# Modulation vectors on TensorE alone: 384 products with one column in place of GpSimd's multiply and add

## What is computed

```
mod   = silu(c) @ w_mod + b_mod        # two layers, 1024 -> 3072: shift, scale, gate
y     = rms_norm(h, gain) * (1 + scale) + shift
h     = h + gate * branch(y)
```

## Time and profile before

| what | us |
|---|---|
| median of 3 runs | 1314.91 |
| lowest and highest of them | 1311.63, 1318.79 |
| the profiled execution's own time | 1313.33 |
| its span in the trace | 1311.5 |
| TensorE busy | 904.6 (69%) |
| VectorE busy | 830.7 (63%) |
| GpSimd busy | 558.0 (43%) |
| ScalarE busy | 257.5 (20%) |

### The profile page before, as it was taken

The page is one execution under the profiler, slowest core; times in us unless marked ns, Lnnn a source line. Parts: engine busy times, 40 slices in busy tenths (PEclk is TensorE's granted clock), DMA queues, the critical chain, the costliest instruction groups (busy, mean ns, idle before and its releaser), DMA issues. The chain is left out here.

```text
span 1311.5 us, 17486 instructions
## 1 busy us (share of the span) xinstructions
PE 904.6 (69%) x6828; PEld 688.4 (52%) x6828; DVE 830.7 (63%) x1942; ACT 257.5 (20%) x515; POOL 558.0 (43%) x440
## 2 busy tenths in 40 slices
PE   6449979997968889687634454434444499659998
PEld 6449958796756657456411131111211288538887
DVE  1975152237978968595478777777765489972311
ACT  3021101103352213221002111011100143412210
POOL 1858777974433433253244445444444034600000
PEclk9769979997879959788756565555655689869999
DMA  9636547758999999999999999999999414212341
GB/s 382 252 129 252 198 176 288 273 210 341 426 420 384 420 418 414 423 423 421 421 421 421 422 420 421 421 421 418 417 420 421 194 67 175 80 64 71 122 148 45
DMA packets 51266, 401.99 MB, mean 307 GB/s; under 512 B 5616, under 2 KB 7920, under 8 KB 8944
## 3 DMA queue, kind: packets, MB, share of 16 engines
q0 software_dynamic: 40320, 293.62, 54.5%
q1 hardware_dynamic: 10000, 104.57, 20.6%
q10 hardware_dynamic: 864, 2.68, 0.5%
HBM read 399.80 MB, written 1.05 MB: 306 GB/s over the span
## 5 line engine op out<-in xcount | busy, mean ns | idle before, releaser
L409 POOL DMA_INDIRECT arena<-uv_dram,arena x192 | 220.8, 1150 | 322.2 <-PE ps L552 276.4
L552 PE MATMUL ps<-arena 128*32 128x256 f32 x1536 | 157.4, 549 | 213.0 <-DVE arena L1410 213.0
L1394 DVE CUSTOM_DVE_ANT_0 arena<-arena 128x1024 f32<-128x1024 f32 x192 | 232.5, 1225 | 98.0 <-DMA arena<-uv_dram,arena 92.2
L552 PEld LDWEIGHTS ps<-arena 128*32 128x32 f32 x1536 | 51.5, 141 | 301.1 <-DVE arena L1410 255.8
L822 PE MATMUL ps<-xn,wring 128*128 128x256 f32 x640 | 147.6, 395 | 17.5 <-DVE arena L1738 9.9
L822 PEld LDWEIGHTS ps<-xn,wring 128*128 128x128 f32 x640 | 127.1, 199 | 38.0 <-issue 18.2
L458 PE MATMUL ps<-xn,wring 128*128 128x128 f32 x1024 | 129.2, 288 | 10.3 <-DMA wring<-units_dram 6.0
L458 PEld LDWEIGHTS ps<-xn,wring 128*128 128x128 f32 x1024 | 125.1, 203 | 18.6 <-issue 8.6
L409 POOL DMA_INDIRECT wring<-uv_dram,arena x64 | 79.2, 1238 | 108.6 <-PE ps L552 98.6
L941 ACT ACTIVATE gel<-dots 128x2 f32<-128x2 f32 x128 | 26.0, 203 | 471.1 <-DVE dots L1394 446.3
L552 PE MATMUL ps<-wring,arena 128*32 128x256 f32 x512 | 50.4, 530 | 72.6 <-DVE arena L1410 72.6
(11 more groups left out here) (244 smaller groups left out, 1319.0 us busy)
## 6 DMA issues: line engine op xcount, KB each, us to landing
wring<-units_dram SPq DMA_DIRECT2D x48, 2048.0 KB, 9.6
arena<-mod_dram POOLq DMA_DIRECT2D x24, 1024.0 KB, 6.2
arena<-uv_dram,arena POOLq DMA_INDIRECT x192, 14.2
hA<-x_t_dram SPq DMA_DIRECT2D x2, 512.0 KB, 5.4
arena<-mem_t_dram ACTq DMA_DIRECT2D x1, 1024.0 KB, 11.5
arena<-keys_dram ACTq DMA_DIRECT2D x2, 512.0 KB, 4.7
wring<-uv_dram,arena POOLq DMA_INDIRECT x64, 14.3
wring<-grp_dram SPq DMA_DIRECT2D x1, 1024.0 KB, 4.8
```

Of the source, the lines that this page charges most:

```text
L409: pool.indirect_dma_start(ring[b], None, uv_d, bass.IndirectOffsetOnAxis(ap=idx[:, n:n + 1], axis=0)).then_inc(sem(f"row_in{b}"), 16)
L552: mm = pe.matmul(acc_ps(q)[G * c:G * (c + 1), :], lhsT=diag[:, s % 2, j, :], rhs=ring[b][:, D + 256 * c:D + 256 * (c + 1)], start=(p == 0 ...
L1394: post(V.tensor_tensor_reduce(out=ring[b][:, 0:D], in0=ring[b][:, 0:D], in1=x_rep[q % 2], scale=1.0, scalar=0.0, op0=ALU.mult, op1=ALU.add ...
```

## The change

GpSimd no longer multiplies or adds. It issues the loads of the chunks, each as soon as TensorE has summed the chunk two before it, and it waits for the last sum ahead of the first gather. TensorE takes the loaded chunk itself as weights: for each of a chunk's two halves of 128 columns, 8 products (one for each block of channels) with one column of `silu_c`, summed in PSUM. `mod_chunk` comes at the same places as before. `mod_p` is gone.

```diff
-MOD_SUMS = 4
@@
-        mod_p = x_rep[1].rearrange("p (s n) -> p s n", s=MOD_SUMS)
@@ GpSimd
-            need(pool, "silu_c")
-            for i in range(MOD_CHUNKS):
-                w = mod_w[:, i % 2]
-                pool.wait_ge(sem(f"mod_in{i % 2}"), 16 * (i // 2 + 1))
-                did(pool, pool.tensor_tensor(w, w, silu_c[:].unsqueeze(2).broadcast_to([P, KB, 256]), ALU.mult), "pool_step")
-                did(pool, pool.tensor_tensor(w[:, 0:4], w[:, 0:4], w[:, 4:8], ALU.add), "pool_step")
-                did(pool, pool.tensor_tensor(w[:, 0:2], w[:, 0:2], w[:, 2:4], ALU.add), "pool_step")
-                if i >= MOD_SUMS:
-                    need(pool, "mod_sum", i - MOD_SUMS + 1)
-                did(pool, pool.tensor_tensor(mod_p[:, i % MOD_SUMS], w[:, 0], w[:, 1], ALU.add), "mod_part")
-                if i + 2 < MOD_CHUNKS:
-                    pool.dma_start(w.rearrange("p k n -> p (k n)"), mod_d[i + 2]).then_inc(sem(f"mod_in{i % 2}"), 16)
+            for i in range(2, MOD_CHUNKS):
+                need(pool, "mod_sum", i - 1)
+                pool.dma_start(mod_w[:, i % 2].rearrange("p k n -> p (k n)"), mod_d[i]).then_inc(sem(f"mod_in{i % 2}"), 16)
+
+            need(pool, "mod_sum", MOD_CHUNKS)
@@ TensorE, mod_chunk(i)
-                need(pe, "mod_part", i + 1)
+                if i == 0:
+                    need(pe, "silu_c")
+                pe.wait_ge(sem(f"mod_in{i % 2}"), 16 * (i // 2 + 1))
                 for j in range(2):
-                    mm = pe.matmul(ps[:, 7, 2 * i + j:2 * i + j + 1], lhsT=mod_p[:, i % MOD_SUMS, j * P:(j + 1) * P], rhs=cst("one"),
-                                   start=True, stop=True)
+                    for k in range(KB):
+                        mm = pe.matmul(ps[:, 7, 2 * i + j:2 * i + j + 1], lhsT=mod_w[:, i % 2, k, j * P:(j + 1) * P], rhs=silu_c[:, k:k + 1],
+                                       start=(k == 0), stop=(k == KB - 1))
                 post(mm, "mod_sum")
```

## The result

| kernel | median, us | ratio to before (95% interval) | first gather, us | span less first gather |
|---|---|---|---|---|
| before | 1316.9 (4 runs) | | 301.4 | 1010.1 |
| changed | 1381.4 (4 runs) | 1.048 (1.043 to 1.052) | 368.3 | 1009.2 |

The forecast was 1378 us, slower, with 1328 to 1404 as the range. The kernel of before ran again beside every group of runs; ratios are always taken within a group.

A forecast was written before the change was run, and what follows sets the result against it. VectorE, then TensorE bound the path to the first gather, then transfers: -35.7 + 71 - 12.6 - 8.6, plus 2.1 and 0.3, gives +16.5 on 1313.3 (1329.8); clock falls add 47 (1376.8); median 1378 us, range 1328 to 1404.

The forecast's parts named there:

- The frame: Transfer engines bound a gather stage of fixed length; the change only shifts its start, the first gather at 301.35 us.
- Part 1, the relief of VectorE: Before L604: without GpSimd's arithmetic VectorE speeds up, so L604 starts at 56.1 us, 35.7 us won, first chunk included.
- Part 2, the price of a record: TensorE's chunks after the first: 28 more records each at 0.11 us, 71 us added; ends 58 and 135 us.
- The rival of cheap weight loads: 128-column weights load at 0.04 us a record, 644 records cost 26 us for 71: 1286 us; chance of faster 0.04.
- Part 3, the waits: TensorE's waits at L684, L458, L729 and L762 close, 12.6 us; half clock after waits goes too, 8.6 us.
- Part 4, loads and gathers: Chunk loads cost 0, at most 3 us; waiting for the last sum before the first gather adds 2.1 and 0.3 us.
- The sum at full clock: First gather 16.5 us later if the clock holds, 1329.8 us; as a rival, median 1331 us, chance 0.18.
- Part 5, the clock: TensorE's one-column chunks act like pauses: 18 clock falls at 2.6 us add 47 us; ends 31 and 74 us.
- The sign "near 0.75": TensorE's granted clock between 92 us and the first gather, expected well below the earlier 0.95, near 0.75.
- The sign "up to 7 us for a chunk at half clock": TensorE's chunks, expected to take 3.5 us at full clock and up to 7 us at half.

The follow-up runs named there:

- e3: Kernel before, but GpSimd begins its arithmetic only when g is there and TensorE's sums stand three steps later: 1297.1 us, ratio 0.979.
- e6: e1_wide, with GpSimd multiplying and adding five times on a scratch buffer, result unused, from about 28 to 70 us: 1365.3 us, ratio 1.037.
- e5: e1_wide with only the first half of each chunk's columns multiplied, 8 products in place of 16: 1293.8 us, ratio 0.984.
- e1_wide: Changed kernel, each product of the modulation passing 128 equal columns of silu_c in place of one: 1334.9 us, ratio 1.009.
- e2: Changed kernel, each chunk in two halves of 16 one-column records, one half after each step from the seventh on: 1344.4 us, ratio 1.015.
- e7: Kernel before, GpSimd's arithmetic begun at g, chunks 0 and 23 on TensorE (128 equal columns), last two chunks early in TensorE's list: 1290.8 us, ratio 0.977.

## Why the prediction was right, point by point

**The frame.** "A fixed time after its start" held to within 5 us over nine kernels. That made it possible to forecast a 1300 us kernel from one moment at 300 us. The forecast had that moment at 364.9 (301.35 + 16.5 + 47), and it came at 368.3.

**Part 1, the relief of VectorE.** Forecast: L604 at 56.1; measured 56.33. The cause is shown from both sides: e3 moves GpSimd's arithmetic in time, e6 adds it back without any use, and L604's place is at 56.35 in the one and 87.3 in the other. One size was off: I priced the eight L1471 at 4.3 us by L1754, and they took 3.3. It did not matter, since the third convolution waited for its input anyway (2.4 us, above).

**Part 2, the price of a record.** Forecast 0.11, measured 0.109 (a chunk, one column), 0.112 (128 columns) and 0.108 to 0.113 on the path (e5). The rival of cheap weight loads is out.

**Part 3, the waits.** Forecast: 12.6 us close. TensorE's waits in the second part went from 14.5 to 2.6 us, so 11.9 did. L458 kept 0.8 us that I had closed. The forecast gave two reasons, a faster VectorE and a slower TensorE. For the wait of 6.8 us at L684 the first alone is enough: VectorE's short convolution took 13.2 us from 170.8 on in the kernel before, and takes 3.1 from 170.9 on now. For the smaller waits nothing parts the two.

**Part 4, loads and gathers.** Landing took 5.2 us in the median and 7.5 at worst, and no chunk waited for its load. `mod_sum` released the first gather.

**The sum at full clock.** It stood at 317.9 us for the first gather; e1_wide, which is that case, has 320.9. Two of these 3 us are the wider products' own (23 chunks x 0.09 us). The forecast had also taken every half clock of before as gone, and e1 kept a fall of 3.4 us right behind the narrow products near 170 us, with no wait there; it is worth up to 1.7 us.

**Part 5, the clock.** This was the bold part, with 47 of the 64 us, and its two factors were choices: 18 falls at 2.6 us. Measured: 19 falls, 102 us at half speed, so 51 us, 2.7 for each. By e1 the first gather moved 47.4 us; with the wider chunks' 2.1 us and the 1.7 us of the fall that e1 kept that makes 51.2, half of the 102. The assumption that a chunk of short columns acts like a pause, which no row could show, is what e1 and e2 have shown. That both factors came out so near is in part luck. Twelve falls, or 24 of 3.1 us each, stood as open as 18, and the price was the least of three rows behind waits, with nothing to say that a fall without a wait would cost the same.

Three readings did not hold. The sign "near 0.75" for the granted clock contradicts the forecast's own sum: 18 falls that each lose 2.6 us are 94 us at half speed, which over some 273 us is 0.83. Measured from 92 to 368.3 us it is 0.82. The sign "up to 7 us for a chunk at half clock" supposed a whole chunk at 0.50, and no chunk took more than 4.8. And the clock did not fall after waits of 5.7 and 6.8 us but within them, at 90.2 and 182.4 us, while the waits ended at 91.8 and 185.6; the time at half clock behind them, on which the price rests, is read rightly.

## What to carry to other kernels

Here a product with one column cost as much as one with 128 (0.109 and 0.112 us a record), and chunks of 3.5 us of them took TensorE to half clock 19 times although it was hardly ever idle; widening the moving operand to 128 equal columns cost 0.1 us a chunk and gave 47 us back. Parting the bursts (e2) gave most of that back too. GpSimd arithmetic that nobody waits for can still set the pace, by slowing VectorE 4.6 to 7.2 times, as in e6: look for one VectorE line with two very different durations, and first try to move GpSimd's work in time (e3) before giving it to an engine that is the bound. When a fixed stage follows, find the one instruction that starts it and forecast that alone.

## What was not expected of the hardware

The size of VectorE's delay beside GpSimd's arithmetic was known from the earlier trace rows; that an instruction with a single tensor input suffers as much was not (L1457 in e6: 0.87 to 6.29 us for four), though the earlier trace rows had a sign of it, 2.22 and 0.87 us for four L1454. And there was the "remote" wait of ScalarE in e7, 6.8 us while the first eight gathers were issued. It stands where the gain of the earlier gathers was lost; that it is the cause is likely by the start of VectorE's product, but no run tested it.
